# The RWKV-7 recurrence of a hybrid decoder step: per-column factors moved into the head-sum weights and onto ScalarE

## The reference: what is computed

```python
kk = heads((k * k_k).astype(f32))
kk = kk / jnp.maximum(jnp.sqrt(jnp.sum(kk * kk, axis=-1, keepdims=True)), 1e-12)
k = k.astype(f32) * (1.0 + (a - 1.0) * k_a.astype(f32))
...
y, s_new = wkv7_scan(rh, heads(decay), kh, vh, -kk, kk * ah, s0)
mu = jnp.mean(y, axis=-1, keepdims=True)
var = jnp.mean(jnp.square(y - mu), axis=-1, keepdims=True)
y = ((y - mu) * lax.rsqrt(var + GN_EPS)).reshape(B, T, D) * ln_w.astype(f32) + ln_b.astype(f32)
bonus = jnp.sum(rh * kh * r_k.astype(f32), axis=-1, keepdims=True) * vh
y = (y + bonus.reshape(B, T, D)) * g.astype(f32)
return y.astype(h.dtype) @ w_o, (s_new.astype(h.dtype), h[:, -1])
```

## Time and profile before

| what | value |
|---|---|
| runs, us | 3300.71, 3296.98, 3295.82; median 3296.98 |
| span of the profiled execution | 3305.9 us (its only time on the page) |
| mean granted TensorE clock | 0.965 |
| PE busy | 3075.8 us (93%) |
| PEld busy | 2867.4 us (87%) |
| DVE busy | 1635.5 us (49%) |
| ACT busy | 908.9 us (27%) |
| POOL busy | 1470.1 us (44%) |

### The profile page before, as it was taken

How to read it: one execution, slowest core, us unless ns; L and a number is a source line. 1 busy time by engine, 2 the same in 40 slices (tenths; PEclk the granted TensorE clock), 3 DMA queues, 4 the chain that set the end, 5 groups by cost and what they waited for, 6 DMA issues and landing times.

```text
span 3305.9 us, 71345 instructions
## 1 busy us (share of the span) xinstructions
PE 3075.8 (93%) x31308; PEld 2867.4 (87%) x31308; DVE 1635.5 (49%) x2059; ACT 908.9 (27%) x1528; POOL 1470.1 (44%) x1107
## 2 busy tenths in 40 slices
PE   7999988989999999979999798888888999999996
PEld 7989856979999999969999577777778999999996
DVE  5023164238666622254112366798823766664125
ACT  4132264232111111134111354444422311111111
POOL 3323310326777733621433355565533477774330
PEclk9999998999999999999999799999979999999998
DMA  3443553222232252114223122212042232324311
GB/s 100 126 130 105 154 172 112 71 90 77 78 106 81 78 180 84 52 65 180 90 89 115 48 76 61 74 48 64 20 175 77 76 85 78 109 78 135 135 42 61
DMA packets 342463, 312.12 MB, mean 94 GB/s; under 512 B 35335, under 2 KB 303059, under 8 KB 341020
## 3 DMA queue, kind: packets, MB, share of 16 engines
q1 hardware_dynamic: 325706, 275.99, 27.5%
q10 hardware_dynamic: 16466, 31.83, 2.5%
HBM read 212.79 MB, written 94.62 MB: 93 GB/s over the span
## 4 chain that ended last, share of the span: by engine, by line
PE 39%; DVE 6%; issue 4%; ACT 3%; POOL 2%; DMA 1%; ACTq 0%; DVEq 0%; POOLq 0%; SPq 0%
PE PS L521 17%; PE PS L688 12%; PE PS L2794 2%; PE PS L2799 2%; PE PS L2861 1%; DVE act_lo L2516 1%; PE PS L2811 1%; PE PS L702 1%; ACT i_nc L3069 1%; DVE f_B L3258 1%; PE PS L2950 1%; POOL f_kk L2732 1%; PE PS L2805 1%; ACT g_N L3071 0%; PE PS L2790 0%
## 5 line engine op out<-in xcount | busy, mean ns | idle before, releaser
L521 PE MATMUL PS<-act_hi,w_hi 128*128 128x344 f32 x1992 | 641.7, 322 | 29.8 <-DVE act_lo L2150 12.9
L521 PE MATMUL PS<-act_lo,w_hi 128*128 128x344 f32 x1992 | 638.1, 320 | 0.0
L521 PE MATMUL PS<-act_hi,w_lo 128*128 128x344 f32 x1992 | 637.6, 320 | 0.0
L502 POOL CAST w_hi<-w_raw 128x1024 fp32r<-128x1024 f32 (+1 forms) x119 | 128.8, 1082 | 1073.7 <-PE PS L521 564.8
L521 PEld LDWEIGHTS PS<-act_hi,w_hi 128*128 128x128 f32 x1992 | 376.5, 189 | 35.3 <-issue 18.2
L521 PEld LDWEIGHTS PS<-act_lo,w_hi 128*128 128x128 f32 x1992 | 376.8, 189 | 0.0
L521 PEld LDWEIGHTS PS<-act_hi,w_lo 128*128 128x128 f32 x1992 | 376.7, 189 | 0.0
L688 PE MATMUL PS<-T,wq_S 128*128 128x258 f32 x2880 | 365.7, 283 | 0.0
L688 PE MATMUL PS<-act_hi,wq_A 128*128 128x258 f32 x1920 | 364.5, 282 | 0.0
L688 PEld LDWEIGHTS PS<-T,wq_S 128*128 128x128 f32 x2880 | 354.4, 189 | 0.0
L688 PEld LDWEIGHTS PS<-act_hi,wq_A 128*128 128x128 f32 x1920 | 305.4, 190 | 0.0
(11 more groups left out here) (597 smaller groups left out, 5983.9 us busy)
## 6 DMA issues: line engine op xcount, KB each, us to landing
hidd<-hid_out SPq DMA_DIRECT2D x44, 516.0 KB, 3.4
w_raw<-in_ffn_w_gate_dram SPq DMA_DIRECT2D x44, 512.0 KB, 4.8
w_raw<-in_ffn_w_up_dram SPq DMA_DIRECT2D x44, 512.0 KB, 6.0
w_raw<-in_ffn_w_down_dram SPq DMA_DIRECT2D x32, 512.0 KB, 4.2
hid_in<-hidd SPq DMA_DIRECT2D x28, 516.0 KB, 7.4
proj<-stage ACTq DMA_DIRECT2D x24, 516.0 KB, 2.7
xT<-xkeep SPq DMA_DIRECT2D x3, 4128.0 KB, 16.6
rw<-z_st SPq DMA_DIRECT2D x24, 516.0 KB, 2.8
```

Of the source, the lines that this page charges most:

```text
L502: nc.gpsimd.tensor_copy(w_hi[:, u, 0:kts, :], w_raw[:, u, 0:kts, :]).then_inc(w_hi_done, 1)
L521: mm = nc.tensor.matmul(PS[:, 3 * u + c, 0:CH], w[:, u, kt, :], x[:, kt, CH * c:CH * c + CH], start=(kt == 0 and part == 0), stop=(kt == k ...
```

## The change

- The factor `k_k` is no longer multiplied into k before the square. ACT squares k itself, and `pkk` uses weights whose rows carry `k_k` squared: `w_kk`, one 128x128 matrix for each of the eight channel tiles, made once in `levels_gpsimd`. So `pkk` is four matmuls of 128 columns with four weight matrices instead of one of 512 columns. `kkn` becomes four DVE instructions of 128x128, each (k times `k_k`) times the norm factor.
- `r_k` goes the same way into `w_rk` (made once at the start of `scan_gpsimd`) and `pbon`.
- The output: ACT applies `ln_w` as scale and `ln_b` as bias to `q_y` in place (`ygn`, four instructions), after `yn` of DVE; it stands between the copies `tV` and `nc` in ACT's list. POOL then adds the bonus (`sum`) and multiplies by g (`o`). The former `f` of ACT and `ea`, `e` of POOL are gone.
- POOL's order is now kp, rk, R, b; sum, o; xad, diag; rkm.
- g has its own two buffers `f_g` and is loaded in turn k for item k, behind the loads of item k + 4 and after `o` of item k - 2. The loads of item k + 4 wait for `b`, `ptV` and `bv` of item k + 2.
- PE's wait for the masks at its start is split, so that it waits for `w_rk` and the cleared state only where it uses them.

```diff
-        for n in "rksavg":
+        for n in "rksav":
...
-        f_e, f_f = room("f_e", [P, 4, GP, P]), room("f_f", [P, 4, GP, P])
+        f_bv, f_g = room("f_bv", [P, 4, GP, P]), room("f_g", [P, 2, GP, P])
+        w_rk = room("w_rk", [P, 2 * GP, P])
...
-        BG = Order(sem("sc_pool"), "kk0:s rrk:s kp:s rk:s R:s b:s be:o o:o xad:i diag:i ea:s e:s rkm:s", AHEAD, -2, ITEMS + 1, ITEMS)
+        BG = Order(sem("sc_pool"), "kp:s rk:s R:s b:s sum:o o:o xad:i diag:i rkm:s", AHEAD, -2, ITEMS + 1, ITEMS)
...
                     if n >= 2:
-                        sp.wait_ge(BG.sem, BG.of("e", n - 2))
-                        sp.wait_ge(BA.sem, BA.of("f", n - 2))
+                        sp.wait_ge(BG.sem, BG.of("b", n - 2))
+                        sp.wait_ge(BP.sem, BP.of("ptV", n - 2))
+                        sp.wait_ge(BV.sem, BV.of("bv", n - 2))
...
+                if 0 <= k < ITEMS:
+                    c, g = item(k)
+                    if k >= 2:
+                        sp.wait_ge(BG.sem, BG.of("o", k - 2))
+                    sp.dma_start(f_g[:, k % 2, :, :], tile(rw[RW["g"] + W4 * g:RW["g"] + W4 * g + W4, P * c:P * c + P])).then_inc(in_g[k % 2], 16)
...
+            kk = vecs[:, VEC["rwkv_k_k"]:VEC["rwkv_k_k"] + 2 * GP]
+            GM.chain(pool, tt(c_kk2[:, :], kk, kk, ALU.mult), "kk2")
+            GM.chain(pool, tt(w_kk[:, :, :], every(m_bd64, 2 * GP), c_kk2[:, :].rearrange("p (k o) -> p k o", o=1).broadcast_to([P, 2 * GP, P]), ALU.mult), "wkk")
...
+            GM.chain(pool, tt(w_rk[:, :, :], every(m_bd64, 2 * GP), vecs[:, VEC["rwkv_r_k"]:VEC["rwkv_r_k"] + 2 * GP].rearrange("p (k o) -> p k o", o=1).broadcast_to([P, 2 * GP, P]), ALU.mult), "wrk")
             GM.chain(pool, pool.memset(q_S[:, :, 0, :, :], 0.0), "S")
...
-                    tt(f_kk[:, :, :], f_in["k"][:, x, :, :], per_pair("rwkv_k_k", g), ALU.mult).then_inc(BG.sem, BG.turn("kk0", s))
...
-                    tt(f_rk[:, :, :], f_in["r"][:, x, :, :], per_pair("rwkv_r_k", g), ALU.mult).then_inc(BG.sem, BG.turn("rrk", s))
...
-                    tt(f_rk[:, :, :], f_rk[:, :, :], f_kp[:, :, :], ALU.mult).then_inc(BG.sem, BG.turn("rk", s))
+                    if s:
+                        pool.wait_ge(BP.sem, BP.of("pbon", s - 1))
+                    tt(f_rk[:, :, :], f_in["r"][:, x, :, :], f_kp[:, :, :], ALU.mult).then_inc(BG.sem, BG.turn("rk", s))
...
                 if 0 <= o:
-                    pool.wait_ge(BV.sem, BV.of("yn", o))
+                    pool.wait_ge(BA.sem, BA.of("ygn", o))
+                    pool.wait_ge(BV.sem, BV.of("bv", o))
...
-                    tt(q_o[o % 2][:, :, :], q_y[:, :, :], f_f[:, o % 4, :, :], ALU.mult).then_inc(BG.sem, BG.turn("be", o))
-                    pool.wait_ge(BG.sem, BG.of("be", o))
-                    tt(q_o[o % 2][:, :, :], q_o[o % 2][:, :, :], f_e[:, o % 4, :, :], ALU.add).then_inc(BG.sem, BG.turn("o", o))
+                    tt(q_o[o % 2][:, :, :], q_y[:, :, :], f_bv[:, o % 4, :, :], ALU.add).then_inc(BG.sem, BG.turn("sum", o))
+                    pool.wait_ge(BG.sem, BG.of("sum", o))
+                    pool.wait_ge(in_g[o % 2], in_g_before[o % 2] + 16 * (o // 2 + 1) + START)
+                    tt(q_o[o % 2][:, :, :], q_o[o % 2][:, :, :], f_g[:, o % 2, :, :], ALU.mult).then_inc(BG.sem, BG.turn("o", o))
...
-                    pool.wait_ge(BV.sem, BV.of("bv", s))
-                    pool.wait_ge(in_b[s % 2], 32 * (s // 2 + 1) + START)
-                    tt(bv, bv, per_pair("rwkv_ln_b", g), ALU.add).then_inc(BG.sem, BG.turn("ea", s))
-                    pool.wait_ge(BG.sem, BG.of("ea", s))
-                    tt(bv, bv, f_in["g"][:, x, :, :], ALU.mult).then_inc(BG.sem, BG.turn("e", s))
...
+            def head_sums(weights, src, g):
+                for q in range(GP):
+                    ins = mm(PS[:, 4, P * q:P * q + P], weights[:, GP * g + q, :], src[:, q, :], start=True, stop=True)
+                return ins
...
-                    sums(m_bd64, f_ns, 4).then_inc(BP.sem, BP.turn("pkk", s))
+                    head_sums(w_kk, f_ns, s % NG).then_inc(BP.sem, BP.turn("pkk", s))
...
-                    sums(m_bd64, f_rk, 4).then_inc(BP.sem, BP.turn("pbon", s))
+                    head_sums(w_rk, f_rk, s % NG).then_inc(BP.sem, BP.turn("pbon", s))
...
-                    act.wait_ge(BG.sem, BG.of("kk0", s))
...
-                    AC(f_ns[:, :, :], f_kk[:, :, :], ACT.Square).then_inc(BA.sem, BA.turn("sq", s))
+                    AC(f_ns[:, :, :], f_in["k"][:, x, :, :], ACT.Square).then_inc(BA.sem, BA.turn("sq", s))
...
+                if live_o:
+                    act.wait_ge(BV.sem, BV.of("yn", o))
+                    for q in range(GP):
+                        c = GP * (o % NG) + q
+                        ins = AC(q_y[:, q, :], q_y[:, q, :], ACT.Identity, scale=vec("rwkv_ln_w", c), bias=vec("rwkv_ln_b", c))
+                    ins.then_inc(BA.sem, BA.turn("ygn", o))
...
-                    for q in range(GP):
-                        ins = AC(f_f[:, s % 4, q, :], f_in["g"][:, x, q, :], ACT.Identity, scale=vec("rwkv_ln_w", GP * g + q))
-                    ins.then_inc(BA.sem, BA.turn("f", s))
...
-                    tt(f_kk[:, :, :], f_kk[:, :, :], f_ns[:, :, :], ALU.mult).then_inc(BV.sem, BV.turn("kkn", s))
+                    for q in range(GP):
+                        ins = stt(f_kk[:, q, :], f_in["k"][:, x, q, :], vec("rwkv_k_k", GP * g + q), f_ns[:, q, :], ALU.mult, ALU.mult)
+                    ins.then_inc(BV.sem, BV.turn("kkn", s))
```

More of the change, by code:

```diff
@@ L2564, in decoder_step @@
         c_mid, c_dm, c_D = room("c_mid", [P, 4, GP]), room("c_dm", [P, GP]), room("c_D", [P, 2, GP])
-        c_oka = room("c_oka", [P, 8], "xT")
+        c_oka, c_kk2 = room("c_oka", [P, 8], "xT"), room("c_kk2", [P, 8], "xT")
+        w_kk = room("w_kk", [P, 2 * GP, P], "xT")
         z_in = {n: room(f"z_{n}", [P, 8, NS]) for n in "ka"}
@@ L2585, in decoder_step @@
         d_bd = {m: nc.alloc_sbuf_tensor_at(f"d_bd{m}", [P, P], F32, offset=free_at["v"] + 2048 + 512 * i) for i, m in enumerate((2, 4, 8, 16))}
-        d_lev = {m: nc.alloc_sbuf_tensor_at(f"d_lev{m}", [P, P], F32, offset=free_at["g"] + 512 * i) for i, m in enumerate((1, 2, 4, 8, 16))}
+        d_lev = {m: nc.alloc_sbuf_tensor_at(f"d_lev{m}", [P, P], F32, offset=free_at["a"] + 512 * i) for i, m in enumerate((1, 2, 4, 8, 16))}
         d_bd[1], d_bd[32], d_bd[64] = ident, m_bd32, m_bd64
@@ L2590, in decoder_step @@
         in_a, in_b, out_st = ([sem(f"sc_{n}{x}") for x in range(2)] for n in ("in_a", "in_b", "out_st"))
+        in_g, in_g_before = (bias_in, gate_w_in), (48, 32)
         AHEAD = {"s": 2, "i": 1, "n": 0, "o": -1}
-        BG = Order(sem("sc_pool"), "kk0:s rrk:s kp:s rk:s R:s b:s be:o o:o xad:i diag:i ea:s e:s rkm:s", AHEAD, -2, ITEMS + 1, ITEMS)
-        BA = Order(sem("sc_act"), "t:s sq:s pe0:s iP:s D:n t4:i ln:s rs:s ysq:o t8:i yln:o yrs:o t16:i tV:s nc:s n:s t32:i tB:s w21:i x21:i t64:i y:n f:s tK:s t2:s rkc:s", AHEAD, -2, ITEMS + 1, ITEMS)
+        BG = Order(sem("sc_pool"), "kp:s rk:s R:s b:s sum:o o:o xad:i diag:i rkm:s", AHEAD, -2, ITEMS + 1, ITEMS)
+        BA = Order(sem("sc_act"), "t:s sq:s pe0:s iP:s D:n t4:i ln:s rs:s ysq:o t8:i yln:o yrs:o t16:i tV:s ygn:o nc:s n:s t32:i tB:s w21:i x21:i t64:i y:n tK:s t2:s rkc:s", AHEAD, -2, ITEMS + 1, ITEMS)
         BV = Order(sem("sc_dve"), "cs:s mid:s cc:s dm:n xs2:i x2:i rhs:n ss:s xs4:i x4:i u:n kkn:s A:s xs8:i x8:i yn:o st:n S:n B:s xs16:i x16:i K:s ct:s xi:s xt:s ak:s bv:s rb:s tr:i", AHEAD, -2, ITEMS + 1, ITEMS)
@@ L2600, in decoder_step @@
         GM = Steps(sem("b_masks"), [f"bd{m}{x}" for m in (2, 4, 8, 16, 32, 64) for x in "ab"] + ["strict"] + [f"{x}{m}" for m in (1, 2, 4, 8, 16) for x in ("lev", "up")]
-                   + "incl cen ones reset S".split())
+                   + "incl cen kk2 wkk ones reset wrk S".split())
         VM = Steps(sem("b_ic_done"), "i0 l0 l1 l2 l3 l4 cen oka".split())
@@ L2642, in scan_sync @@
                             sp.wait_ge(stored[u], 16 * (S0 + 8 + GP // 2 * (g + 1)) + START)
-                    for name in "vg":
-                        sp.dma_start(f_in[name][:, n % 2, :, :], part(name)).then_inc(in_b[n % 2], 16)
+                    sp.dma_start(f_in["v"][:, n % 2, :, :], part("v")).then_inc(in_b[n % 2], 16)
                 if n == 1:
@@ L2826, in scan_tensor @@
                     pe.wait_ge(BA.sem, BA.of("tV", n))
+                    if n == 0:
+                        pe.wait_ge(GM.sem, GM["S"] + START)
                     if n:
@@ L2954, in scan_tensor @@
                     pe.wait_ge(BA.sem, BA.of("tB", s))
-                    sums(m_bd64, f_rk, 4).then_inc(BP.sem, BP.turn("pbon", s))
+                    if s == 0:
+                        pe.wait_ge(GM.sem, GM["wrk"] + START)
+                    head_sums(w_rk, f_rk, s % NG).then_inc(BP.sem, BP.turn("pbon", s))
                     pe.wait_ge(BG.sem, BG.of("R", s))
@@ L3089, in scan_scalar @@
                     if live_o:
```

(11 more changed lines are left out.)

17 lines of the change are left out of this document (7 added, 10 removed).

## The result

| kernel | median of the runs, us | span of the profiled execution | granted TensorE clock |
|---|---|---|---|
| before | 3298.85 (3295.82 to 3300.77, 4 runs) | 3305.9 | 0.965 |
| after | 3336.32 (3332.2 to 3342.58, 4 runs) | 3333.9 | 0.953 |

The changed kernel is slower: ratio 1.011, 95% interval 1.0089 to 1.013, about 37 us by the medians and 28.0 us between the two profiled executions (that of before was a long one; its median here has a fourth run beside the three that the prediction had). 3336 us lies outside the predicted range of 3276 to 3312.

What follows compares the result with a forecast made beforehand. PE was taken to bound the kernel, turn length set between `pAS` and `w21`. Terms -4.0 - 0.9 + 1.6 + 1.2 = -2.1 us, carried over to the 3296.98 us median, gave 3295 us; range 3276 to 3312.

Steps and rivals of the forecast that it cites:

- G2: PE's wait for `B` before `pN`, 13.6 us in 12 turns, can go but becomes a longer wait for `w21`.
- the whole stage cannot give back more than that: In the turns of 32 to 35 us, PE stands 3 to 4 us; claimed as the limit of the gain.
- four rivals: POOL queue not binding 3269 us, 0.25; longer queue 3312, 0.17; bare weight loads 3324, 0.06; no effect 3297, 0.07.
- the second rival: `sum` to `diag` on POOL, turns 1 to 13: queue longer than forecast, turns 1.0 us longer, 3312 us; chance 0.17.
- G1: Ahead of `yn`, turns 1 to 13: square wait 11.7 us plus about 5 us of transposes, 16.7 us, 1.28 each.
- The head sums: `pkk` and `pbon` as four matmuls each: taken at 0, bounds -0.12 to +0.9 us each.
- `kkn`: Four DVE instructions before `A`, `b` and `B`: about 0.25 us more, counted 0, at most +0.5 us a turn.
- `S` and `B`: DVE products freed of `be` beside them: `S` gives back 0.84 us and `B` 1.1 us.
- ACT and POOL: `ygn` delays `sum`, then `o`, `xad`, `diag`, for which `w21` waits: `w21` 0.31 us a turn earlier, 4.0 us in 13.
- the delay: `sum` behind `ygn` in ACT's queue begins 2.87 us later after `yn` than `be` did.
- Turns without cover: Turn 0 gains 0.9 us, turn 14 loses 1.6 us, the chain after the last item loses 1.2 us.
- at the end, where 1.2 were to be lost: After the last item `yn`, product, `o`, store and reload form one chain: 1.65 us more, less part of a collision.

Runs made afterwards that it cites:

- e10: Kernel before with only the key square changed, a second measurement (meant to have idle products, but ran without): 3295.24 us, ratio 0.9981 to before.
- e7: Kernel before with only the key square changed (`kk0` gone, ACT squares k, `pkk` through `w_kk`, `kkn` as four DVE instructions): 3294.79 us, ratio 0.997 to before.
- e8: Kernel before with ACT's copy `tB`, ahead of `w21`, made in eight pieces of 128x64 instead of one of 128x512: 3323.02 us, ratio 1.0057 to before.
- e3: Changed kernel with `pbon` again as one product with the plain block matrix, `r_k` left out of the bonus: 3332.78 us, ratio 1.0107 to before.
- e1: Changed kernel with `xad` and `diag` moved ahead of `sum` and `o` in POOL's order: 3295.16 us, ratio 0.9984 to before.
- e4: Only the output part of the change, key and bonus factors back on POOL with plain head sums: 3333.63 us, ratio 1.0094 to before.
- e2: Changed kernel with six idle products on PE ahead of its wait for `w21`: 3295.79 us, ratio 0.9979 to before.
- e5: Changed kernel with `xad`, `diag` ahead of `sum`, `o` on POOL and six idle products on PE before the `w21` wait: 3290.66 us, ratio 0.9956 to before.
- e9: e5 with the first two weight loads of the output product issued by SyncE one turn earlier: 3285.49 us, ratio 0.995 to before.

## Why the prediction was wrong

**The step that failed** stands in the first part: "After `pT64` the timeline has PE without a gap up to the next turn's `pAS`, so the length of a turn is set between `pAS` and `w21`." The stretch behind `pT64` was taken as fixed, 7.75 us, because PE never waits in it. It has no gap, but its length hangs on the clock, and the clock on the stand ahead of it: 115.4 us became 145.0 over turns 0 to 13. These +29.6 us are more than the whole difference of 28.0 us between the two executions, and 29.0 of them are busy time of PE (109.6 us became 138.6): not waiting, but the same products slower. So the sentence that "G2 turns from a wait for `B` into a longer wait for `w21`" was right and wrongly priced: 15.1 us of wait moved into one place were booked as an exchange at par. The hint was in the trace of before, in the turns that I did not open: turn 5 has 7.75 us, turn 12 has 9.30 at granted 0.82. For the same reason "the whole stage cannot give back more than that" was no bound: PE's busy time is not fixed either. I worked one calm turn through and counted the others like it. None of the four rivals had the clock in it, so the range had no place for the result either; 3336 us is outside it on the slow side, beyond the second rival's 3312, which got the sign but not the mechanism (`diag` ended 7.9 us after `sum` began in turn 5, not over 9.5). Nor did DVE keep the door there, as that rival had it: the add behind `ct` (L3288, 0.42 us undisturbed) took 1.38 us and ended 0.29 us after `xad`, so it waited for POOL.

**The key square.** The wait is gone. Alone it brings 9.8 us and, in e10, 6.8; the term G1 said 11.7 us for the wait in turns 1 to 13 and 16.7 with the transposes. Over these turns `w21` comes 8.2 us earlier in e7, half of that.

**The head sums.** Taken at 0: 1.16 us for eight passes against 1.12, in the earlier trace rows for the one product. Right; bare weight loads do not occur.

**`kkn`.** 1.13 us, +0.45 where I had +0.25. Nothing waits for it first.

**`S` and `B`.** By line, shortest, median and longest in ns, against the earlier trace rows:

```profile
L3274 DVE TENSOR_TENSOR f_B<-f_b,f_iP x16: 651/684/693, 1854.5 to 2381.6; 128x512 f32<-128x512 f32 x16
L3270 DVE TENSOR_TENSOR q_S<-q_S,c_D x16: 424/426/427, 1920.0 to 2451.5; 128x256 f32<-128x256 f32 x16
L3285 DVE TENSOR_TENSOR i_C<-i_nc,m_lev x16: 1492/2414/3652, 1858.9 to 2387.2; 128x1280 f32<-128x1280 f32 x16
```

Both as forecast, and `ct`'s median is 1.0 us shorter.

**ACT and POOL.** `sum` begins 2.88 us after `yn` ended (2.87 was said to be the delay), the queue from `sum` to `diag`'s end takes 7.9 us in turn 5 and 8.2 in turn 13, somewhat less than my 8.6 and 9.1. `w21` came 6.4 us earlier over turns 1 to 13 where I had 4.0. The mechanism, to which I gave most weight, was right: `diag` releases `w21` in each of the turns 1 to 13, 0.08 to 0.15 us after its end. The size was right in part by luck. As means of the 13 turns, `yn` ends 0.55 us earlier in the turn where I had 1.28, the delay is 2.75 us (2.87), 2.44 us of slack are used up (2.53), and `be` to `diag`'s end, 8.29 us, became 8.05, shorter by 0.24 where I had it 0.63 longer. Two errors of 0.73 and 0.87 us a turn nearly cancel.

**Turns without cover.** Turn 0 gained 1.1 us (0.9 said). Turn 14 lost 5.2 instead of 1.6: `ygn` is in its path as said, and it began behind turn 13's long stand, with `yn` 3.4 us later in the turn than before (15.02 against 11.61 us); the granted clock from its start to `yn` was 0.73, against 1.00 before. The values of a single turn are weak evidence, though: turn 0 takes 21.7 to 25.8 us up to `w21` and turn 14 takes 22.9 to 30.0 us in the executions of this study. The 3.3 us gained at the end, where 1.2 were to be lost, and the 3.9 us lost at the start are inside the scatter too, and I do not put them down to the change.

**What stays open.** Which of several stands of nearly one length is followed by the half clock: 1.65 us in turn 5 of the changed kernel was not, 1.50 us in turn 5 of e8 was. Nor does length alone decide: in e3 a stand of 2.71 us (turn 8) is followed by 7.75 us at full clock and one of 1.07 us (turn 10) by 9.31 us at 0.82. What is shown is how often: 0 to 6 of fourteen stretches are over 8.5 us behind stands of 1.06 us (before, e1, e7, e10), eight behind 1.50 us (e8), nine or ten where most stands are longer (after, e3, e4). What decides in the single turn is not shown. Output part (+31.9 us) and key square (-9.8 us) do not add up to the whole (+37 us) by the medians; the bonus part never ran alone, and the intervals are too wide to say whether the parts act on each other. And the key square alone, at 3294.8 us, is near the whole change with its two cures, 3290.7 us.

## What to carry to other kernels

Count where PE's waits stand, not only their sum: several short ones moved into one long one can cost more than they save, since the products behind it may run at 1.2 GHz (here +29.6 us of duration for 15.1 us of wait moved into one place). So price a stretch that has no gap by its duration in every turn of the trace and by its granted clock beside it, not by one clean turn. When the next product on PE waits for a slow chain elsewhere, put what that chain doesn't need behind it in the other engine's list (e1), or fill the stand with products that nobody reads (e2).

## What had not been expected of the hardware

- A copy that is 0.44 us later, with a stand of 1.50 instead of 1.06 us, was followed by 4.5 us more for the same 198 products in turn 5, and by 12.2 us more in the turns 0 to 13 together (e8); six products without use brought 40 us (e2).
- The same kernel had six slow stretches behind a stand of 1.06 us in one execution and none in another (e7, e10).
- Eight PSUM copies of 128x64 on ACT take 1.03 us together, one of 128x512 takes 0.59.
- Two weight loads held SyncE for 15.63 us when issued right behind the stores of the samples' state, and for 1.19 us one turn earlier (e5, e9); in the kernel before they held it for 15.61 us. That the stores in front are the cause was not tried.
